# Queries and values of the next token tile projected between attention steps, with the ratio of sums on GpSimd

## Chip, cores and metric

The kernel runs on one core of a Trainium2 chip. The time is the device time of one execution, in microseconds. Three runs of the kernel before gave 947.82, 948.0 and 953.27; their median is 948.0.

## What is computed

One layer of a hybrid decoder for 512 prompt tokens and 64 sample tokens (8 sequences of 8), all float32. The part of the reference that matters here:

```python
mod = jax.nn.silu(c) @ w_ada + b_ada                      # adaLN: (shift, scale, gate) twice
h = rms_norm(x, g_pre_mix) * (1 + sc1) + sh1
zq, zk, zv, zu, zs = jnp.split(h @ w_in, ...)             # five column groups of 512
a = diff_attn_prompt(q, k, v, lam, slopes)                # 8 heads, two components of 32 each
#   s = q.k - slope * dist, masked;  p = softmax(s);  a = (p[0] - lam * p[1]) @ v
a = rms_norm(a, g_subln) * (1 - lam_init)
u = jax.nn.gelu(zu); vs = layer_norm(jax.nn.gelu(zs)); s_out = spatial_gating(u, vs)
mix = concatenate([a, s_out]) @ w_out                     # then sample attention, merge, 16 experts
```

## The kernel before, in words

The program is hand-scheduled: each engine has its own instruction stream, in order, tied to the others by semaphores. Four functions matter. `condition` norms x and runs adaLN round 0. `project` multiplies the normed tokens `hT` with the five column groups of `w_in`, in the order of `WIN_ORDER` (k, s, u, v, q), each for `NT` = 5 token tiles: four of 128 prompt tokens (8 matmuls of 128 x 512) and one of the 64 sample tokens (the 8 matmuls go to the lower and the upper half of the array's columns in turn, L776; VectorE adds the halves, L677 and L678). ScalarE copies each group out of PSUM, k, q and s groups are transposed or mixed behind it (`post`) and copied by VectorE (L667). adaLN rounds 1 and 2 (`ada_round`, L509, 64 short matmuls each, four 2 MB units of `w_ada`) run behind the groups named in `ADA_AFTER`. `attend_prompt` is prompt attention: 32 steps, tile i = 0 to 3 outside and head h = 0 to 7 inside; tile i has 128 (i + 1) keys. `attend_sample` is attention over the paged cache for the 8 sample sequences.

All large transfers go into a ring of slots of 2 MB (`L.ring`, 0 to 5). `STATIC` lists the weight units in the order in which SyncE's queue asks for them, with the slot of each (`ADA`, `WIN`); SyncE waits in order until the use before in the slot is over. `load_pages` (L794) on GpSimd gathers half a sequence's keys or values into a slot.

A step of attention, before: ScalarE has placed q of this tile into four zero-padded copies (`place_q`, L871), so that each of the two components is a matmul over all 128 partitions. TensorE writes two score banks (L958), two pairs in turn. VectorE adds the distance bias, takes the maximum and writes to one of three buffer pairs `pb` (L933), negates both maxima (L938); ScalarE takes exponentials with sums (L884). VectorE makes the ratio of the sums times -lambda (L909, L910) and combines the two components (L912), one head behind. TensorE transposes the weights two heads behind (L966), ScalarE copies them (L894), TensorE multiplies with the values three heads behind (L977), into bank 6 or 7 by tile. Behind head 4 of the next tile, `finish` divides, norms and stores the tile's eight heads in one go, VectorE waiting for a power on GpSimd (L816, L817). The order of the work in a step is that of the code:

```python
for n in range(N + 3):            # TensorE
    if n < N: ...                 # two score matmuls of head n, once s_read says the bank pair is free
    if 2 <= n < N + 2: ...        # transposes of head n - 2, once a_ready and at_done allow
    if n >= 3: ...                # value matmuls of head n - 3, once at_done allows
```

TensorE begins attention only when all five groups are projected (L947 to L949). GpSimd asks for six page loads at the start of attention (L846 to L851): keys of sequences 0 and 1, values of sequence 0, into slots 0 to 5.

Of the kernel before, what the change touches and what calls it, by code (L numbers as in the profile page):

```python
# [17 lines left out]
ALU = mybir.AluOpType  # L18
# [5 lines left out]
P = 128  # L24
# [5 lines left out]
NT = 5  # L30
# [126 lines left out]
def chain(eng, sem, start=0):  # L157
# [3 lines left out]
    def link(ins):  # L161
# [18 lines left out]
STATIC = [("ada", 0, j, s) for j, s in enumerate(ADA[0])] + [("win", 0, c, s) for c, s in enumerate(WIN)] + \  # L180
         [("ada", r, j, s) for r in (1, 2) for j, s in enumerate(ADA[r])]
# [14 lines left out]
def expert_slot(e, kind):  # L196


    q = 3 * e + kind
    slot = EXPERT[q % 8]  # L200
    return slot, STATIC_USES[slot] + (slot in W_OUT) + q // 8 + 1


class Program:
# [332 lines left out]
    def project(self, block):  # L537
# [5 lines left out]
        bn_done, rs_done, vs_ready, u_done, k_out, v_out, vs_out, ln_in = (  # L543
            self.sem(n) for n in ("bn_done", "rs_done", "vs_ready", "u_done", "k_out", "v_out", "vs_out", "ln_in"))
        dchain, pchain = self.sem("dve_chain_b"), self.sem("pool_chain_b")
        lam_in, lam_sum, lam_exp = (self.sem(n) for n in ("lam_in", "lam_sum", "lam_exp"))
        self.grp_done, self.evac_done, self.post_ev, self.posts = grp_done, evac_done, post_ev, 3 * NT
        summed = self.sem("summed")
        half = L.mix[0:NS, 3, 0:512]
# [3 lines left out]
        E = [L.at(L.X + 512 * i, 512) for i in range(4)]  # L553
        lng, lnb = L.at(L.V + 1536, 512), L.at(L.V + 2048, 512)
        groups = [(c, t) for c in WIN_ORDER for t in range(NT)]
        posts = [n for n, (c, t) in enumerate(groups) if c in "skq"]
# [3 lines left out]
        v_o = [o["v_prompt"][0, 0, t * P:(t + 1) * P].rearrange("t h d -> t (h d)") for t in range(4)] + \  # L560
            [o["v_sample"][0].rearrange("b t h d -> (b t) (h d)")]
# [8 lines left out]
        def _(sp):  # L570
# [10 lines left out]
            sp.wait_ge(self.mod_out, 16 * 2)  # L581
            sp.wait_ge(self.mod_outs, 16 * 8)
# [26 lines left out]
        def _(act):  # L609
            for n, (c, t) in enumerate(groups):  # L610
                r = rows(t)
                if c == "q" and t == 0:
                    act.wait_ge(lam_sum, 1)
                    act.activation(self.lam[:, 130:132], self.lam[:, 128:130], ACT.Exp).then_inc(lam_exp, 1)
# [4 lines left out]
                if n >= 4:  # L619

                    cb, tb = groups[n - 4]
                    if cb in "skq":
                        act.wait_ge(post_done, posts_to(n - 4))
# [8 lines left out]
                elif c == "v":  # L632
                    if t == 0:
                        act.wait_ge(post_done, posts_to(s0 + 4))
# [1756 lines left out]
```

## Time and profile before

| | us |
|---|---|
| median of three runs | 948.0 |
| the execution that was profiled | 947.89 |
| its span | 946.2 |
| TensorE busy in the span | 841.9 |
| VectorE busy | 346.4 |
| ScalarE busy | 208.9 |
| GpSimd busy | 118.8 |
| granted clock of TensorE, mean | 0.94 of full |
| bytes moved | 249.15 MB, 263 GB/s |

The span is what the hardware profiler saw of one execution, from the first to the last instruction; the time of the same execution is 1.7 us longer. Busy time of TensorE contains matmuls at a reduced clock. Condition takes about the first 40 us, projection goes to about 227, prompt attention to 334, sample attention to some 500, and merge and experts take the rest.

### The profile page before, as it was taken

Reading aid. Unit: us, or ns where it says so; the run is one execution under the profiler, and the core shown is the slowest. Engines: PE = TensorE matmul, PEld = TensorE weight load, DVE = VectorE, ACT = ScalarE, POOL = GpSimd, SP = SyncE. Lnnn points to the kernel's source line nnn. Section 1 sums busy time; section 2 is a strip of 40 time slices with the busy share of each in tenths; the row PEclk is TensorE's granted clock in tenths of the full one; section 3 lists DMA queues with packets and bytes.
Section 4 is the critical chain, followed back from the end, with each engine's and each line's share of the span. In section 5 each row is a group of like instructions: output and inputs, shape, how many; then the busy total and the mean of one; then the engine's idle time right before and its main releaser. Section 6 shows DMA issues by size and latency. Waiting matters only on the chain. (4 is left out here: it accounts for less than half of the span.)

```text
span 946.2 us, 12198 instructions
## 1 busy us (share of the span) xinstructions
PE 841.9 (89%) x4720; PEld 436.2 (46%) x4720; DVE 346.4 (37%) x843; ACT 208.9 (22%) x436; POOL 118.8 (13%) x190
## 2 busy tenths in 40 slices
PE   4699999997789679999988999479999999999995
PEld 3244444333555455665654455344444444444431
DVE  2304332104778545555451364442103011101137
ACT  4001001103666324333330211110101111101122
POOL 1300000002200112222120010001000000000044
PEclk8899999999779879999998998669999999999998
DMA  8996203635910047999797951508888999999973
GB/s 312 365 306 246 89 17 112 259 147 183 410 42 1 1 164 285 413 417 428 298 367 263 340 217 34 200 23 354 335 340 325 401 425 401 396 428 381 409 281 119
DMA packets 36709, 249.15 MB, mean 263 GB/s; under 512 B 4377, under 2 KB 5785, under 8 KB 23218
## 3 DMA queue, kind: packets, MB, share of 16 engines
q1 hardware_dynamic: 22834, 155.17, 41.8%
q0 software_dynamic: 9376, 81.47, 22.0%
q10 hardware_dynamic: 4448, 11.82, 3.8%
q8 instruction: 34, 0.56, 0.2%
q14 instruction: 17, 0.14, 0.0%
HBM read 231.91 MB, written 16.53 MB: 263 GB/s over the span
## 5 line engine op out<-in xcount | busy, mean ns | idle before, releaser
L770 PE MATMUL ps<-sb 128*128 128x512 f32 x320 | 142.8, 602 | 1.8 <-DVE sb L410 1.8
L2054 PE MATMUL ps<-sb 128*128 128x512 f32 (+1 forms) x256 | 112.9, 594 | 0.0
L770 PEld LDWEIGHTS ps<-sb 128*128 128x128 f32 x320 | 60.1, 192 | 75.7 <-issue 74.0
L1206 PE MATMUL ps<-sb 128*128 128x128 f32 x512 | 66.1, 284 | 18.8 <-ACT sb L1075 9.3
L1206 PEld LDWEIGHTS ps<-sb 128*128 128x128 f32 x512 | 57.6, 145 | 32.4 <-issue 18.3
L1978 DVE TENSOR_TENSOR sb<-sb,ps 128x512 f32<-128x512 f32 (+1 forms) x16 | 10.9, 684 | 160.3 <-PE ps L2054 87.1
L2044 PE MATMUL ps<-sb 128*128 128x512 f32 x144 | 66.4, 616 | 1.0 <-ACT sb L1896 0.9
L2079 PE MATMUL ps<-sb 128*128 128x512 f32 x144 | 63.5, 594 | 0.0
L1726 PE MATMUL ps<-sb 128*128 128x512 f32 x128 | 58.4, 616 | 3.9 <-DVE sb L1485 3.9
L2054 PEld LDWEIGHTS ps<-sb 128*128 128x128 f32 (+1 forms) x256 | 42.0, 167 | 34.0 <-issue 34.0
L958 PE MATMUL ps<-sb 128*128 128x128 f32 (+3 forms) x128 | 50.1, 526 | 3.2 <-ACT sb L871 3.2
L2051 PE MATMUL ps<-sb 128*64 128x512 f32 x112 | 49.6, 595 | 0.0
L1122 DVE COPY sb<-ps 128x512 f32<-128x512 f32 x64 | 41.2, 686 | 21.0 <-PE ps L1206 20.6
L1873 POOL DMA_INDIRECT sb<-h_rows,ints x16 | 15.0, 938 | 249.0 <-PE ps L2016 209.6
L884 ACT ACTIVATE sb<-sb 128x128 f32<-128x128 f32 (+3 forms) x64 | 35.4, 554 | 40.1 <-DVE sb L938 39.9
L2044 PEld LDWEIGHTS ps<-sb 128*128 128x128 f32 x144 | 27.6, 197 | 33.6 <-issue 31.7
L1075 ACT ACTIVATE sb<-ps 128x512 f32<-128x512 f32 x64 | 34.9, 595 | 33.9 <-PE ps L1206 33.5
L1726 PEld LDWEIGHTS ps<-sb 128*128 128x128 f32 x128 | 24.9, 198 | 34.5 <-issue 32.3
L2079 PEld LDWEIGHTS ps<-sb 128*128 128x128 f32 x144 | 26.7, 190 | 30.3 <-issue 30.1
L1989 DVE COPY sb<-ps 128x512 f32<-128x512 f32 (+1 forms) x16 | 11.1, 692 | 73.7 <-PE ps L2079 56.2
L1219 PE MATMUL ps<-sb 128*32 128x512 f32 (+1 forms) x320 | 36.5, 530 | 0.0
L933 DVE CUSTOM_DVE_ANT_0 sb<-ps,sb 128x128 f32<-128x128 f32 (+3 forms) x64 | 30.0, 489 | 14.7 <-PE ps L958 14.0
(297 smaller groups left out, 1018.6 us busy)
## 6 DMA issues: line engine op xcount, KB each, us to landing
sb<-in_w_gate SPq DMA_DIRECT2D x16, 2048.0 KB, 19.4
sb<-in_w_up SPq DMA_DIRECT2D x16, 2048.0 KB, 9.5
sb<-in_w_down SPq DMA_DIRECT2D x16, 2048.0 KB, 14.2
sb<-in_w_ada SPq DMA_DIRECT2D x12, 2048.0 KB, 15.5
sb<-in_w_in SPq DMA_DIRECT2D x5, 2048.0 KB, 24.6
y_rows<-sb SPq DMA_DIRECT2D x9, 512.0 KB, 15.5
sb<-in_w_out SPq DMA_DIRECT2D x2, 2048.0 KB, 21.2
sb<-in_x_prompt SPq DMA_DIRECT2D x4, 512.0 KB, 5.1
```

The costliest lines, as they stand in the source:

```text
L770: last = pe.matmul(PS[:, n % 4, :], L.hT[:, k, t * P:t * P + P], w[:, k, :], start=k == 0, stop=k == KC - 1)
L884: act.activation(pb[n % 3][j][:, 0:w], pb[n % 3][j][:, 0:w], ACT.Exp, bias=nm[:, q:q + 1], accum_out=sums[:, q:q + 1]).then_inc(exp_done, 1)
L958: pe.matmul(PS[:, 2 * (n % 2) + j, 0:P * (i + 1)], qz[i % 2][:, h // 2, 2 * (h % 2) + j, :], L.kT[:, h // 2, 0:P * (i + 1)], start=True, s ...
L1075: act.activation(kt[ch % 2][:, h, :], PS[:, h, :], ACT.Copy).then_inc(kt_act, 1)
L1122: dve.tensor_copy(kt[ch % 2][:, h, :], PS[:, h, :]).then_inc(kt_dve, 1)
L1206: last = pe.transpose(PS[:, h, P * g:P * g + P], kp[:, 4 * (ch % 2) + g, P * h:P * h + P], L.cst("ident"))
L1219: last = pe.matmul(bank[32 * h:32 * h + 32, 0:512 if ch < 4 else NS], qst[par][:, h, :], rhs, start=True, stop=True)
L1726: last = pe.matmul(PS[:, proj_bank(i, c), :], mixT[i % 2][:, k, :], w[:, k, :], start=k == 0, stop=k == KC - 1)
L2044: last = pe.matmul(PS[:, 0, :], x[:, k, :], w_gate[:, k, :], start=k == 0, stop=k == KC - 1)
L2051: last = pe.matmul(PS[n:P, 0, :], x[:, k, :], w_gate[:, k, :], start=k == 0, stop=k == KC - 1)
L2054: last = pe.matmul(PS[0:n, 1, :], x[:, k, :], w_up[:, k, :], start=k == 0, stop=k == KC - 1)
L2079: last = pe.matmul(PS[:, 5 + c, :], hT[:, k, :], w[:, k, 512 * c:512 * c + 512], start=k == 0, stop=k == FC - 1)
```

## The change

Projection keeps k, s and u; adaLN rounds 1 and 2 move up behind groups s2 and u1, with their own order of ring slots, and the weights of v and q are loaded behind them. Groups q and v move into `attend_prompt`. Tile 0 is projected ahead of the first head; q of tile t = i + 1 is spread over steps 0 to 2 of the eight heads of tile i, transposed in step 3, and v of tile t over steps 4 to 7 (`beside`, `product`, `turn`). All of these go through PSUM bank 7 (`bank_of`); values now gather in bank 6 alone. Value outputs are stored by SyncE's queue instead of ScalarE's.

The scores read the 32 partitions of q and k of one component directly, so `place_q` is gone. VectorE computes bias minus score and its minimum, which is the negated maximum, so the negation is gone, and ScalarE's exponential takes a scale of -1. The ratio of the sums is made by GpSimd, with three small operations. The combination is two heads behind instead of one, transposes three and value matmuls four, and there are four buffer pairs, which lie in ring slot 3. The norm of a tile is spread over heads 3, 4 and 5 of the next. The work on page numbers, distance bias and lambda sums moves from group v0 to u2. Of the six page loads three are asked for at the start of attention, slots 2 and 5 near its end, and slot 3 when the last value matmul is done.

```diff
-ADA = [[0, 1, 2, 3], [3, 4, 5, 0], [3, 4, 5, 0]]
-WIN = [4, 5, 0, 1, 2]
+ADA = [[0, 1, 2, 3], [1, 2, 3, 4], [1, 2, 3, 4]]
...
-ADA_AFTER = [("v", 2), ("q", 2)]
+ADA_AFTER = [("s", 2), ("u", 1)]
...
+STATIC = [("ada", 0, j, s) for j, s in enumerate(ADA[0])] + [("win", 0, c, s) for c, s in enumerate(WIN[:3])] + \
+         [("ada", r, j, s) for r in (1, 2) for j, s in enumerate(ADA[r])] + \
+         [("win", 0, 3 + c, s) for c, s in enumerate(WIN[3:])]
+ATTEND_SLOT = 3
...
+    return 3 * NT + len(BESIDE) * t + (c == "v")
...
+    t, k = n // H + 1, n % H
+    if n >= 4 * H:
+        return []
+    return [[("q", t, 0), ("q", t, 1)], [("q", t, 2)], [("q", t, 3)], [("turn", t, 0)],
+            [("v", t, 0)], [("v", t, 1)], [("v", t, 2)], [("v", t, 3)]][k]
...
+        slot = L.ring[ATTEND_SLOT]
+        pb = [[slot[:, 1024 * i + 512 * j:1024 * i + 512 * j + 512] for j in range(2)] for i in range(4)]
+        at = [self.E[2 + i].rearrange("p (b q) -> p b q", b=4) for i in range(2)]
...
-        qz = [L.at(n0 + 2048 * i, 2048).rearrange("p (h g q) -> p h g q", h=HP, g=4) for i in range(2)]
...
+        def bank_of(c, t):
+            return 6 if (c, t) == ("v", 0) else 7
...
+            pool.wait_ge(self.lam_sum, 1)
+            pool.wait_ge(grp_done, 3 * NT)
+            self.load_pages(pool, self.ck, 0, 0, K_SLOT[0][0], 0)
             pool.wait_ge(self.ada_done, 3)
-            pool.wait_ge(self.grp_done, 5 * NT)
-            for k, (cache, b, slots) in enumerate(((self.ck, 0, K_SLOT[0]), (self.ck, 1, K_SLOT[1]),
-                                                   (self.cv, 0, V_SLOT))):
-                for half in range(2):
-                    self.load_pages(pool, cache, b, half, slots[half], 2 * k + half)
+            self.load_pages(pool, self.ck, 0, 1, K_SLOT[0][1], 1)
+            self.load_pages(pool, self.cv, 0, 0, V_SLOT[0], 2)
...
+            for m in range(N):
+                q = 2 * m
+                pool.wait_ge(exp_done, q + 2)
+                link(pool.tensor_tensor(cf[:, q:q + 1], sums[:, q + 1:q + 2], minus, ALU.pow))
+                link(pool.tensor_tensor(cf[:, q:q + 1], cf[:, q:q + 1], sums[:, q:q + 1], ALU.mult))
+                if m == 0:
+                    pool.wait_ge(lam_made, 1)
+                pool.tensor_tensor(cf[:, q:q + 1], cf[:, q:q + 1], lam[:, 133:134], ALU.mult).then_inc(cf_ready, 1)
+                if m % H == 3 and m > H:
+                    pool.wait_ge(ss_ready, m // H)
+                    self.power(pool, link, ss, H, P, 1.0 / DV, ss_power)
+                if m == N - 4:
+                    pool.wait_ge(grp_done, group_at("q", 4) + 1)
+                    self.load_pages(pool, self.ck, 1, 0, K_SLOT[1][0], 3)
+            pool.wait_ge(grp_done, group_at("v", 4) + 1)
+            self.load_pages(pool, self.cv, 0, 1, V_SLOT[1], 4)
+            pool.wait_ge(pv_done, N)
+            self.load_pages(pool, self.ck, 1, 1, K_SLOT[1][1], 5)
...
-            place_q(0)
...
+            def project(c, t):
+                r, src = rows(t), PS[0:rows(t), bank_of(c, t), :]
+                act.wait_ge(grp_done, group_at(c, t) + 1)
+                if t == 4:
+                    act.wait_ge(self.summed, 4 + (c == "v"))
+                if c == "q":
...
+                    act.activation(E[t % 2][0:r], src, ACT.Copy, scale=DQK ** -0.5).then_inc(evac_done, 1)
...
+            for n in range(N + 3):
                 if n < N:
-                    act.wait_ge(m_ready, n + 1)
                     w = P * (work[n][0] + 1)
                     for j in range(2):
                         q = 2 * n + j
-                        act.activation(pb[n % 3][j][:, 0:w], pb[n % 3][j][:, 0:w], ACT.Exp, bias=nm[:, q:q + 1],
-                                       accum_out=sums[:, q:q + 1]).then_inc(exp_done, 1)
-                if n % H == 3 and n // H < 3:
-                    place_q(n // H + 1)
-                if n >= 2:
-                    m = n - 2
+                        act.wait_ge(s_read, q + 1)
+                        act.activation(pb[n % 4][j][:, 0:w], pb[n % 4][j][:, 0:w], ACT.Exp, bias=nm[:, q:q + 1],
+                                       scale=-1.0, accum_out=sums[:, q:q + 1]).then_inc(exp_done, 1)
+                if n >= 3:
+                    m = n - 3
...
+                for c, t, part in beside(n):
+                    if c != "turn" and part == 3:
+                        project(c, t)
...
+            def turned(t):
+                r = rows(t)
+                dve.wait_ge(post_done, 2 * NT + t + 1)
+                dve.tensor_copy(L.qT[:, :, t * P:t * P + r],
+                                PS[:, 7, :].rearrange("p (h t) -> p h t", h=HP)[:, :, 0:r]).then_inc(post_ev, 1)
...
-                dve.wait_ge(exp_done, 2 * m + 2)
-                link(dve.reciprocal(cf[:, q:q + 1], sums[:, q + 1:q + 2]))
-                link(dve.scalar_tensor_tensor(cf[:, q:q + 1], sums[:, q:q + 1], lam[:, 133:134], cf[:, q:q + 1],
-                                              ALU.mult, ALU.mult))
+                p1, p2 = pb[m % 4][0][:, 0:w], pb[m % 4][1][:, 0:w]
+                dve.wait_ge(cf_ready, m + 1)
                 dve.scalar_tensor_tensor(p1, p2, cf[:, q:q + 1], p1, ALU.mult, ALU.add).then_inc(a_ready, 1)
...
-                        dve.tensor_tensor_reduce(out=pb[n % 3][j][:, 0:w], in0=PS[:, 2 * (n % 2) + j, 0:w],
-                                                 in1=self.dist_bias[:, h, 384 - P * i:512], scale=1.0, scalar=-3e38,
-                                                 op0=ALU.add, op1=ALU.max,
-                                                 accum_out=mx[:, q + j:q + j + 1]).then_inc(s_read, 1)
-                    dve.wait_ge(s_read, 2 * n + 2)
-                    dve.tensor_scalar_mul(nm[:, q:q + 2], mx[:, q:q + 2], -1.0).then_inc(m_ready, 1)
-                if n >= 1:
-                    weights(n - 1)
-                if n % H == 4 and n // H >= 1:
-                    finish(n // H - 1)
-            finish(3)
+                        dve.tensor_tensor_reduce(out=pb[n % 4][j][:, 0:w], in0=PS[:, 2 * (n % 2) + j, 0:w],
+                                                 in1=self.dist_bias[:, h, 384 - P * i:512], scale=-1.0, scalar=3e38,
+                                                 op0=ALU.add, op1=ALU.min,
+                                                 accum_out=nm[:, q + j:q + j + 1]).then_inc(s_read, 1)
+                if n >= 2:
+                    weights(n - 2)
+                for c, t, part in beside(n):
+                    if c == "turn":
+                        turned(t)
+                    elif t == 4 and part == 3:
+                        summed(c)
+                if n < N and n >= H:
+                    if n % H == 3:
+                        taken(n // H - 1)
+                    if n % H == 4:
+                        squares(n // H - 1)
+                    if n % H == 5:
+                        normed(n // H - 1)
...
+            def product(c, t, part):
+                number = WIN_ORDER.index(c)
+                w = L.ring[WIN[number]].rearrange("p (k n) -> p k n", k=KC)
+                bank = bank_of(c, t)
+                if part == 0:
+                    if t == 0:
+                        pe.wait_ge(self.ring_full[WIN[number]], 16 * fills("win", 0, number))
+                    else:
+                        pe.wait_ge(post_ev, 2 * NT + t + (c == "v"))
+                    if c == "q" and t >= 2:
+                        pe.wait_ge(evac_done, group_at("v", t - 1) + 1)
+                if t < 4:
+                    for k in (2 * part, 2 * part + 1):
+                        last = pe.matmul(PS[:, bank, :], L.hT[:, k, t * P:t * P + P], w[:, k, :],
+                                         start=k == 0, stop=k == KC - 1)
+                else:
+                    for c0, k in ((0, part), (NS, part + KC // 2)):
+                        last = pe.matmul(PS[c0:c0 + NS, bank, :], L.hT[:, k, SEQ:TOK], w[:, k, :],
+                                         start=part == 0, stop=part == KC // 2 - 1)
+                if part == 3:
+                    last.then_inc(grp_done, 1)
...
+            def turn(t):
+                r = rows(t)
+                pe.wait_ge(evac_done, group_at("q", t) + 1)
+                for h in range(HP):
+                    last = pe.transpose(PS[:, 7, P * h:P * h + r], E[t % 2][0:r, P * h:P * h + P],
+                                        L.cst("ident", r)[:, 0:r])
+                last.then_inc(post_done, 1)
             pe.wait_ge(self.mod_sb, 9)
-            for n in range(N + 3):
+            for part in range(4):
+                product("q", 0, part)
+            for part in range(4):
+                product("v", 0, part)
+            turn(0)
...
+                        pe.wait_ge(post_ev, 2 * NT + i + 1)
                     for j in range(2):
-                        pe.matmul(PS[:, 2 * (n % 2) + j, 0:P * (i + 1)], qz[i % 2][:, h // 2, 2 * (h % 2) + j, :],
-                                  L.kT[:, h // 2, 0:P * (i + 1)], start=True, stop=True).then_inc(s_done, 1)
-                if 2 <= n < N + 2:
-                    m = n - 2
+                        r = 32 * (2 * (h % 2) + j)
+                        pe.matmul(PS[:, 2 * (n % 2) + j, 0:P * (i + 1)], L.qT[r:r + 32, h // 2, P * i:P * i + P],
+                                  L.kT[r:r + 32, h // 2, 0:P * (i + 1)], start=True, stop=True).then_inc(s_done, 1)
+                if 3 <= n < N + 3:
...
+                for c, t, part in beside(n):
+                    if c == "turn":
+                        turn(t)
+                    else:
+                        product(c, t, part)
+                if n >= 4:
...
+                        pe.wait_ge(evac_done, group_at("v", i) + 1)
+                        if i:
+                            pe.wait_ge(o_read, i)
```

## Rows read from the trace of the kernel before

**Rows 1.** The page: span and count of instructions.
```profile
span 946.2 us, 12198 instructions
```

**Rows 2.** TensorE's timeline: start, length (us), line, operation, count [idle before]; projection.
```profile
98.16 7.13 PE L770 MATMUL ps<-sb 128*128 128x512 f32 x16
...
145.75 20.87 PE L770 MATMUL ps<-sb 128*128 128x512 f32 x48
166.55 7.05 PE L509 MATMUL ps<-sb 128*9 128x512 f32 x64
...
180.60 3.65 PE L776 MATMUL ps<-sb 128*64 128x512 f32 x16
...
198.02 0.60 PE L752 MATMUL ps<-sb 128*128 128x128 f32 x4
...
229.91 2.90 PE L958 MATMUL ps<-sb 128*128 128x128 f32 x12 [3.20 <-ACT sb L871]
```

**Rows 3.** Windows: stretch, length, busy PE, PEld, DVE, ACT, POOL; PEclk, DMA, GB/s.
```profile
229.91:327.76 97.85, 81.11 (x528) 52.37 (x528) 72.88 (x274) 55.76 (x172) 12.46 (x18) 0.85 0.35 139
293.65:309.31 15.66, 15.66 (x113) 9.46 (x111) 13.52 (x40) 9.79 (x25) 0.09 (x1) 1.00 0.00 1
```

**Rows 4.** Waits of TensorE in attention: us in total, times, longest.
```profile
PE ps L966 <- DVE sb L912: 8.7, 6, 3.9
PE ps L977 <- ACT sb L894: 7.8, 7, 2.4
```

**Rows 5.** TensorE's timeline in attention, heads with 128, 256 and 512 keys.
```profile
242.90 0.74 PE L958 MATMUL ps<-sb 128*128 128x128 f32 x4
...
244.27 1.13 PE L958 MATMUL ps<-sb 128*128 128x256 f32 x4
245.24 0.27 PE L966 MATMUL ps<-sb 128*128 128x128 f32 x1
245.51 0.34 PE L977 MATMUL ps<-sb 128*64 128x64 f32 x4
...
306.06 1.98 PE L958 MATMUL ps<-sb 128*128 128x512 f32 x4
307.89 0.60 PE L966 MATMUL ps<-sb 128*128 128x128 f32 x4
308.42 0.97 PE L977 MATMUL ps<-sb 128*64 128x64 f32 x16
309.31 1.98 PE L958 MATMUL ps<-sb 128*128 128x512 f32 x4
```

**Rows 6.** Windows behind attention and in sample attention, columns as in rows 3.
```profile
327.76:335.97 8.21, 0.01 (x2) 0.03 (x1) 3.66 (x7) 0.00 (x0) 1.83 (x2) 0.74 0.00 0
...
290.00:336.00 46.00, 32.92 (x249) 20.52 (x248) 30.22 (x86) 18.54 (x47) 3.66 (x4) 0.88 0.00 1
380.00:460.00 80.00, 74.39 (x954) 48.51 (x952) 44.22 (x108) 30.09 (x53) 19.78 (x34) 1.00 1.00 417
```

**Rows 7.** TensorE's timeline in sample attention: eight passes on four column quarters.
```profile
380.38 1.06 PE L1219 MATMUL ps<-sb 128*32 128x512 f32 x8
```

**Rows 8.** Groups by form in attention: busy us, mean ns | idle before, releaser.
```profile
L884 ACT ACTIVATE sb<-sb 128x512 f32<-128x512 f32 x16 | 11.4, 714 | 16.4 <-DVE sb L938 16.4
L933 DVE CUSTOM_DVE_ANT_0 sb<-ps,sb 128x512 f32<-128x512 f32 x16 | 10.9, 690 | 5.1 <-PE ps L958 4.7
L912 DVE SCALAR_TENSOR_TENSOR sb<-sb 128x512 f32<-128x512 f32 x8 | 6.0, 752 | 0.3
L894 ACT ACTIVATE sb<-ps 128x512 f32<-128x512 f32 x8 | 4.5, 576 | 1.2 <-PE ps L966 1.2
```

**Rows 9.** Groups by form, GpSimd, whole span.
```profile
L801 POOL DMA_INDIRECT sb<-in_cache_k,ints x16 | 15.9, 994 | 13.6 <-POOL ints L798 12.4 <-issue 1.2
...
L330 POOL TENSOR_TENSOR sb<-sb 128x1 f32<-128x1 f32 x4 | 2.2, 552 | 0.3
...
L600 POOL TENSOR_SCALAR sb<-sb 128x1 f32<-128x1 f32 x4 | 0.8, 190 | 61.3 <-DVE sb L685 61.3
```

More of the change, by code:

```diff
@@ L552, in project @@
         k_outs = [k_out] + [self.sem(f"k_out{i}") for i in range(1, 4)]
-        E = [L.at(L.X + 512 * i, 512) for i in range(4)]
+        E = self.E = [L.at(L.X + 512 * i, 512) for i in range(4)]
         lng, lnb = L.at(L.V + 1536, 512), L.at(L.V + 2048, 512)
-        groups = [(c, t) for c in WIN_ORDER for t in range(NT)]
-        posts = [n for n, (c, t) in enumerate(groups) if c in "skq"]
+        groups = [(c, t) for c in WIN_ORDER[:3] for t in range(NT)]
+        posts = [n for n, (c, t) in enumerate(groups) if c in "sk"]
         mv = self.stats[:, 8:10]
@@ L727, in _ @@
                     post(n - 1)
-            post(len(groups) - 1)
         @block.tensor
@@ L840, in attend_prompt, with _ @@
         N = len(work)
+        E = self.E
+        v_o = [o["v_prompt"][0, 0, t * P:(t + 1) * P].rearrange("t h d -> t (h d)") for t in range(4)] + \
+            [o["v_sample"][0].rearrange("b t h d -> (b t) (h d)")]
+        def bank_of(c, t):
+            return 6 if (c, t) == ("v", 0) else 7
+        @block.sync
+        def _(sp):
+            for t in range(NT):
+                sp.wait_ge(evac_done, group_at("v", t) + 1)
+                sp.dma_start(v_o[t], L.v[0:rows(t), t, :]).then_inc(v_out, 16)
+            sp.wait_ge(v_out, 16 * NT)
+            sp.wait_ge(self.mod_out, 16 * 2)
+            sp.wait_ge(self.mod_outs, 16 * 8)
         @block.gpsimd
@@ L859, in _ @@
                 pool.dma_start(unused[:, WIDE - 2, 2, cols], L.mix[0:HALF, 4, 0:512]).then_inc(zeroed, 16)
-            for i in range(4):
-                pool.wait_ge(ss_ready, i + 1)
-                self.power(pool, link, ss, H, P, 1.0 / DV, ss_power)
+            pool.wait_ge(self.mod_sb, 9)
+            pool.memset(minus, -1.0).then_inc(minus_set, 1)
+            pool.wait_ge(minus_set, 1)
+            for m in range(N):
[16 more added lines that the diff above has]
+            self.load_pages(pool, self.ck, 1, 1, K_SLOT[1][1], 5)
+            pool.wait_ge(ss_ready, 4)
+            self.power(pool, link, ss, H, P, 1.0 / DV, ss_power)
             pool.wait_ge(zeroed, 64)
@@ L951, in _ @@
+            turn(0)
+            for n in range(N + 4):
                 if n < N:
                     i, h = work[n]
+                    if n == 0:
+                        pe.wait_ge(evac_done, 3 * NT)
                     if n >= 2:
```

149 lines of the change are left out of this document (75 added, 74 removed).

## The prediction

> **What bounds the kernel now.** I began with the span [rows 1] and then read TensorE's timeline through the projection and prompt attention, the only two stages that the diff touches. Up to the end of column group q TensorE does not stop: a full group (one column group, one token tile) takes 6.93 us, a third of the 20.8 between the starts at 145.75 and 166.55; a group of the 64 sample tokens 3.65 us, a transposition of q 0.6 us, an adaLN round 7.0 us [rows 2]. The first score matmul stands at 229.91. From there to the last value matmul, at 327.76, attention takes 97.85 us; TensorE is busy for 81.1 of them, at a mean granted clock of 0.85, and VectorE for 72.9 [rows 3]. So two things cost time there: TensorE waits (for VectorE's weights and for ScalarE's copies, 16.5 us together [rows 4]), and after such waits it runs part of the work at 1.2 GHz instead of 2.4. In the stretch where the clock is 1.00, TensorE is busy all of the time: 15.66 of 15.66 us [rows 3]. Attention is therefore TensorE's as soon as nothing stalls it, and the question is how much work TensorE has after the change.
>
> **TensorE's own work in attention, at full clock.** By starts of neighbouring rows at 1.00 [rows 5]: the two scores of a head take 0.74 us at 128 keys, 0.97 at 256, 1.83 at 512; by the half way between, 1.40 at 384. Transposes take 0.27 at one block and 0.53 at four; value matmuls 0.3 (of 0.34 with their modelled end) and 0.89; the two tiles between go by even steps. Four tiles of 8 heads: scores 8 x 4.94 = 39.5, transposes 8 x 1.6 = 12.8, values 8 x 2.4 = 19.0. Sum 71 us, against the 97.85 that it takes now: 27 us are stall and low clock.
>
> **Ahead of attention.** Groups u3 and u4 end at 145.75 today [rows 2]. Both adaLN rounds now run ahead of that point: 2 x 7.0 gives 159.7. They need their weights: each unit is 2.1 MB, and the queue moves 417 GB/s when it is full [rows 6], 5 us a unit. Round 1 takes the place at which s3 starts today, 98.2. Round 2's four units are asked for when it ends, at 105, and take 20 us, to 125 or so. From the start of s3 to the end of u4 it is 47.6 us today, of which u2 to u4 are 2 x 6.93 + 3.65 and a mixing of 1, 18.5: so TensorE comes to round 2 at 105 + 29 = 134. Some 8 us of slack. The weights of q are asked for at the end of round 2, 141, with nothing ahead in the queue but v's; needed at 159.7, so hidden with 10 us to spare. If that cover went, each late unit would cost up to 5 us. Then q0 and v0, 13.9 us, the transposition 0.6, VectorE's copy 0.7 and two hand-overs of 0.3: the first scores start at about 175.2, 54.7 us earlier than now. This also removes the q placing on ScalarE, whose place is the 3.2 us before 229.91 [rows 2].
>
> **What is moved into attention.** Six full groups (q and v of tiles 1 to 3), 41.6 us; two sample groups, 7.3; four transpositions by starts, some 2. Sum 51 us. With 71 this is 122 us of TensorE work between the first score and the last value. For the seams I add 5 us, an estimate: 28 parts each begin behind small matmuls and show 0.1 us of a weight load, and the last four steps drain as now.
>
> **Scores without placed q.** A score now reads 32 partitions, and the two of a head read different quarters of the array's rows and write different banks. No row of before has two matmuls on different row quarters. One bound: they run one after the other, as now: nothing gained. Other bound: as matmuls on different column quarters do, eight passes of 512 columns in 1.06 us, where two matmuls on the full array, four passes, take 1.83 [rows 5, 7]; likewise the 16 records of a sample group, on column halves, take half the time of a full group [rows 2]. With fewer keys the four weight loads of a head hold it at the 0.74 that 128 keys take already. So 0.74, 0.76, 0.9, 1.06 in place of 0.74, 0.97, 1.40, 1.83: 8 x 1.48 = 11.8 us less. I take this one: the column rows show the array running separate quarters at once. The end for the range keeps the other.
> The Trainium skill ("TensorE: Matmul & The Clock Gate", Part 3 on packing small matmuls) gives 3.07 times for four row tiles of 32 rows; by that the two scores would share their time much as the column rows have it. Against the change it says ("TensorEngine Tiling (Array Packing)", Key Properties) that a change of tiling mode drains the engine. Every head already switches between full and half-column matmuls, and [rows 5] has that in the prices.
>
> **VectorE, ScalarE, GpSimd.** Per head at 512 keys VectorE keeps two score reads of 0.69 and one combination of 0.75 [rows 8], with gaps 2.3 us; the reciprocal, the small product and the negation leave it. Eight heads: 18.4; with ten operations more of 512 columns at 0.69 (the copy of qT, four for the sample sums, five for the head norm) and small ones, 26 us. TensorE in the same eight heads of the last tile: 8 x (1.06 + 0.53 + 0.89) + 7.3 + 0.6 = 27.7. Close, but under; in the other tiles far under. ScalarE: two exponentials of 0.71, a copy of 0.58 and an evacuation as long every fourth head [rows 8], some 2.2 us a head. GpSimd: a power of 0.55 and two products of 0.2 with their hand-overs, 1.3 us a head [rows 9]. The ratio is ready about 5 us after the head's first score, and the combination, two heads later, asks for it at 8 or more; a load of pages in GpSimd's queue holds it 2 us longer [rows 9], still covered. Cost of the ratio on GpSimd: nothing; if the cover went, 1.3 us a head, 40 in all at the most.
> Bank 7 carries every moved group. After a group's last part TensorE still has values, the next scores and transposes, 1.3 to 3.2 us, and ScalarE's evacuation needs 0.8 of it; the head norm is spread over three heads, so the stalls of four heads [rows 4] end, and with them the low clock.
>
> **Behind attention.** The tail (8.2 us to the first transposes of the sample part [rows 6]) keeps its operations. GpSimd's last page load sits ahead of the norm's power, 2 us beside VectorE's 2.4: hidden. Three loads of pages move from the start of attention to its end. DMA is idle for the last 46 us now [rows 6], so slots 2 and 5 land before the sample part or with it, and slot 3, first read for the second half of the second sequence, at its start; the sample part's own rate of 417 GB/s between 380 and 460 says that bytes left over for it would cost 5 us a load. 4.2 MB ahead of the bias table may hold VectorE: 1 us. All later stages start by as much earlier, since none of their loads is asked for before.
>
> **Sum.** 122 - 11.8 + 5 = 115 us of attention from 175.2: end at 290, 37.5 earlier than 327.76; less 1 for the table. 946.2 - 36.5 = 909.7 of span. The execution profiled took 947.9 us, 1.7 more than its span, and the median of the runs is 948.0, so the two agree: 911 us.
>
> **Rivals.** (a) *The two scores stay serial*: 122 + 5 = 127, end at 302, 25 us gained: 923. For it: no row shows row quarters at once. (b) *Hand-over through bank 7*: ScalarE takes exp(n) and the copy ahead of the evacuation, and TensorE waits at eight evacuations and four transpositions, 1 to 1.5 us each, 12 to 16 on top of (a): 937. For it: in-order queues. Against: the 1.3 us of other work in between. (c) *The change of place buys nothing*: weights or ratio late enough to eat the 25 to 37 us, 947. That wants 5 late units or 1 us at every head. Against it: [rows 6, 9]. (d) *The clock*: with 32 of 128 rows in use in the scores the granted clock stays at 1.2 GHz. Each us of TensorE work at that level takes two. All of it: 122 more, against 25 gained, 1045 us. From 25 of the 122 us at the low level on, one fifth, it is slower than before. For it: the mean of 0.85 now [rows 3]; against: that follows waits, and products of full height lie between the scores.
>
> **How the numbers follow.** Chances: forecast 0.48, (a) 0.32, (b) 0.10, (c) 0.05, (d) 0.05. 911 us. The range goes from the forecast without seams and table (905, less 2 for waits that I count and that may vanish) to (a) with 3 us more: 903 to 926. Within 1% (about what a measurement can tell) means 938.5 to 957.5: (c), a little. Faster 0.9, same 0.05, slower 0.05.
>
> **What the profile after would show.** First score row near 175; last value row near 290 (302 for (a)); the granted clock of the stretch between at 0.97 or more (0.7 or less for (d)); TensorE busy over 95% of it; the scores of a head at 512 keys 1.1 us apart from the transposes (1.8 for (a)); no wait of TensorE for ScalarE's evacuations over 5 us in total (12 or more for (b)); none of VectorE for GpSimd's ratio; the sample part unchanged in length. Wrong would be the forecast if VectorE were busy over 95% of the last tile, or a projection waited for in_w_in or in_w_ada.

## The result, and the profile after

| | before | after |
|---|---|---|
| median, us | 947.9 (947.2 to 953.3, 4 runs) | 912.1 (909.8 to 914.0, 4 runs) |
| execution profiled: time / span, us | 947.9 / 946.2 | 909.8 / 907.8 |
| mean granted clock | 0.94 | 0.953 |

The ratio is 0.961, with a 95% interval of 0.957 to 0.965. Two later measurements of the same kernel, with the kernel before beside it each time, gave 904.9 and 906.9 (ratios 0.954 and 0.956). The prediction was 911.

TensorE's timeline at the three points that the prediction named: start, length, line, operation, count [idle before].

```profile
173.13 0.60 PE L1056 MATMUL ps<-sb 128*128 128x128 f32 x4
174.60 0.49 PE L1077 MATMUL ps<-sb 32*128 32x128 f32 x4 [0.87 <-DVE sb L952]
...
280.08 1.90 PE L1103 MATMUL ps<-sb 128*64 128x64 f32 x32
295.96 4.30 PE L1332 MATMUL ps<-sb 128*128 128x128 f32 x20 [13.98 <-PEq L282]
```

The first scores start at 174.60 (229.91 in [rows 2]) and the last value matmul ends at 281.98. Behind it stands the first disagreement with the forecast: a gap of 13.98 us, where the kernel before has 8.20 [rows 6]. Its releaser is TensorE's own sequencer at L282, the end of the block, and no data.

Windows of the kernel after (columns as in [rows 3]): all of attention, then the gap.

```profile
174.60:281.98 107.38, 106.24 (x672) 53.30 (x672) 59.04 (x186) 53.56 (x168) 39.75 (x106) 1.00 0.20 66
281.98:295.96 13.98, 0.01 (x1) 0.03 (x1) 3.65 (x6) 0.00 (x0) 3.53 (x4) 0.65 0.71 279
```

TensorE is busy for 106.2 of 107.4 us (99%), at a granted clock of 1.00; before it was 81.1 of 97.9 at 0.85 [rows 3]. Its waits in that stretch, in us, times, longest, are three:

```profile
PE ps L1077 <- DVE sb L952: 0.9, 1, 0.9
PE ps L1056 <- ACT sb L912: 0.6, 1, 0.6
PE ps L1085 <- DVE sb L966: 0.4, 1, 0.4
```

against 16.5 us of [rows 4]. The stalls are gone, and the low clock with them.

Heads with 128, 256 and 512 keys in TensorE's timeline:

```profile
187.70 0.49 PE L1077 MATMUL ps<-sb 32*128 32x128 f32 x4
188.12 0.33 PE L1085 MATMUL ps<-sb 128*128 128x128 f32 x1
188.28 1.88 PE L1042 MATMUL ps<-sb 128*128 128x512 f32 x4
190.10 0.34 PE L1103 MATMUL ps<-sb 128*64 128x64 f32 x4
...
195.70 0.70 PE L1077 MATMUL ps<-sb 32*128 32x256 f32 x4
196.33 0.33 PE L1085 MATMUL ps<-sb 128*128 128x128 f32 x1
...
248.98 1.13 PE L1077 MATMUL ps<-sb 32*128 32x512 f32 x4
250.04 0.55 PE L1085 MATMUL ps<-sb 128*128 128x128 f32 x3
```

From start to next start the two scores of a head take 0.42, 0.63 and 1.06 us, where [rows 5] had 0.74, 0.97 and 1.83. The part of a moved group (L1042) takes 1.8 us and stands between the transposes and the values of other heads.

### The profile page after: what moved, and what is told of

It is laid out like the page before. It is cut to its first block and busy times, and to the rows that moved or that the text cites. A ratio compares the mean times of both kernels' runs of the same rounds, so it can differ in the third digit from the quotient of the medians.

```text
span 907.8 us, 12182 instructions
## 1 busy us (share of the span) xinstructions
PE 815.8 (90%) x4720; PEld 415.2 (46%) x4720; DVE 327.6 (36%) x747; ACT 199.5 (22%) x420; POOL 151.6 (17%) x287
## 5 line engine op out<-in xcount | busy, mean ns | idle before, releaser
L1332 PEld LDWEIGHTS ps<-sb 128*128 128x128 f32 x512 | 57.1, 144 | 37.7 <-issue 24.1
L1042 PE MATMUL ps<-sb 128*128 128x512 f32 x128 | 59.2, 597 | 0.1
L768 PEld LDWEIGHTS ps<-sb 128*128 128x128 f32 x192 | 36.2, 193 | 45.7 <-issue 44.2
L2170 PEld LDWEIGHTS ps<-sb 128*128 128x128 f32 x144 | 27.6, 197 | 33.6 <-issue 31.7
L1852 PEld LDWEIGHTS ps<-sb 128*128 128x128 f32 x128 | 24.9, 198 | 34.7 <-issue 32.4
L2205 PEld LDWEIGHTS ps<-sb 128*128 128x128 f32 x144 | 26.7, 190 | 30.3 <-issue 30.1
```

The source lines that it names most:

```text
L768: last = pe.matmul(PS[:, n % 4, :], L.hT[:, k, t * P:t * P + P], w[:, k, :], start=k == 0, stop=k == KC - 1)
L1042: last = pe.matmul(PS[:, bank, :], L.hT[:, k, t * P:t * P + P], w[:, k, :], start=k == 0, stop=k == KC - 1)
L1332: last = pe.transpose(PS[:, h, P * g:P * g + P], kp[:, 4 * (ch % 2) + g, P * h:P * h + P], L.cst("ident"))
L1852: last = pe.matmul(PS[:, proj_bank(i, c), :], mixT[i % 2][:, k, :], w[:, k, :], start=k == 0, stop=k == KC - 1)
L2170: last = pe.matmul(PS[:, 0, :], x[:, k, :], w_gate[:, k, :], start=k == 0, stop=k == KC - 1)
L2205: last = pe.matmul(PS[:, 5 + c, :], hT[:, k, :], w[:, k, 512 * c:512 * c + 512], start=k == 0, stop=k == FC - 1)
```

## The experiments

Where no range stands beside a time, it is of one run; the others are medians. "Gap" is the time from the end of the last value matmul to the first transposes of the sample part; "attention" is from the first score matmul to the end of the last value matmul.

### The gap behind attention: loads, stores or traffic

**e1_loads_behind.** GpSimd's last two page loads are issued behind the end of the block.

```diff
-            self.load_pages(pool, self.cv, 0, 1, V_SLOT[1], 4)
             pool.wait_ge(pv_done, N)
-            self.load_pages(pool, self.ck, 1, 1, K_SLOT[1][1], 5)
...
+            self.load_pages(pool, self.cv, 0, 1, V_SLOT[1], 4)    # attend_sample, GpSimd
+            self.load_pages(pool, self.ck, 1, 1, K_SLOT[1][1], 5)
             refill(0, 0, True, 6)
```

> The last two page loads of prompt attention (slots 5 and 3) are asked for behind the barrier, ahead of the first refill of sample attention. Theory L (the barrier ahead of sample attention ends only when GpSimd's page loads have landed): the gap between the last value matmul and the first transposes of sample attention falls from 13.98 us to 8.2 as before, the span from 907.8 to 902 to 904. Theory V (SyncE's wait for the last value store holds the barrier, its bytes queued beside the loads) also gives 8 to 10 here; only the next run tells it from L. Theory N (the gap is the semaphore clearing or code of the longer program): it stays at 14 and the span at 907 or more. If both loads come too late for sequences 0 and 1, TensorE waits in sample attention and gives some of it back: 2 to 5 us.

Measured: 899.9 us (899.1 to 903.3, 4 runs), ratio 0.950 (0.947 to 0.952). The gap row of its timeline:

```profile
290.43 4.22 PE L1332 MATMUL ps<-sb 128*128 128x128 f32 x24 [8.20 <-PEq L282]
```

The gap is 8.20 us again, to a hundredth that of the kernel before. The span of the profiled execution, 898.4 us, is shorter than the 902 to 904 that I expected; the kernel after itself ran 5 to 7 us faster in its two later measurements (e5_after_again, e12_after_third), so only e11_loads_again, which has both kernels on one chip, prices the edit.

**e2_no_store_wait.** SyncE's wait for the value stores is taken out of the block; ScalarE waits for them at the end of sample attention.

```diff
-            sp.wait_ge(v_out, 16 * NT)          # attend_prompt, SyncE
...
+            act.wait_ge(self.v_out, 16 * NT)    # attend_sample, ScalarE, last
```

> SyncE's wait for the five value stores moves from the end of prompt attention to the end of sample attention (on ScalarE); the page loads stay where they are. Theory V: the gap behind the last value matmul falls from 14.0 to 8 to 9 us. Theory L: it stays at 14.0, within 0.5.

Measured: 904.9 us. The gap stays:

```profile
296.66 5.27 PE L1333 MATMUL ps<-sb 128*128 128x128 f32 x24 [14.46 <-PEq L282]
```

So it is not the stores.

**e3_other_traffic.** As e1_loads_behind, but SyncE asks for two units of w_ada, 4.2 MB that nothing uses, when the last value matmul is done, and GpSimd waits for them behind the end of the block.

```diff
+            sp.wait_ge(pv_done, N)
+            for s in (3, 5):
+                sp.dma_start(ring[s], a["w_ada"]...).then_inc(self.spare, 16)
...
+            pool.wait_ge(self.spare, 32)        # attend_sample, ahead of the two page loads
```

> As e1, and SyncE's queue asks for 2 x 2 MB of w_ada into the same slots 3 and 5 when the last value matmul is done; nothing waits for them before the barrier, GpSimd waits for them behind it. The loaded values are not used. Theory L (only GpSimd's own transfers hold the barrier): the gap is 8.2 to 8.7. Theory C (any traffic on the DMA engines at that moment holds the barrier, since something that the barrier needs is queued behind it): 13 to 17 us, about 10 us of transfer and the rest.

Measured: 905.2 us. Windows of its gap, then waits of TensorE and of GpSimd:

```profile
281.50:289.80 8.30, 0.00 (x0) 0.03 (x1) 3.66 (x6) 0.00 (x0) 1.85 (x2) 0.61 0.87 336
```

```profile
PE ps L1338 <- PEq L282: 8.3, 1, 8.3
```

```profile
POOL ints L795 <- DMA sb<-in_w_ada: 8.4, 1, 8.4
```

The DMA engines are 0.87 busy through the gap, and it is still 8.3 us: the transfers run on past the end of the block and hold nobody but the wait that names them. Bytes in flight on SyncE's queue do not lengthen it; page loads in flight on GpSimd's do. In the kernel after the engines fall idle shortly before TensorE goes on (windows of 1 us, last columns DMA share and GB/s):

```profile
291.00:292.00 1.00, 0.00 (x0) 0.00 (x0) 0.00 (x0) 0.00 (x0) 0.00 (x0) 0.50 0.95 410
292.00:293.00 1.00, 0.00 (x0) 0.00 (x0) 0.00 (x0) 0.00 (x0) 0.00 (x0) 0.50 0.24 98
293.00:294.00 1.00, 0.00 (x0) 0.00 (x0) 0.00 (x0) 0.00 (x0) 0.00 (x0) 0.50 0.00 0
```

VectorE's last work there ends at 288.0; the loads end at about 292.3, and TensorE starts 3.7 us later. The other profiles agree. In all nine that have the two loads ahead of the end of the block, TensorE starts 3 to 4 us after the DMA engines fall idle. The gap is 12.61 us in e8_ratio_vector, where GpSimd issues the value load 5.3 us before the last value matmul ends, 13.98 us in the kernel after (3.0 us before), and 15.92 us in e10_depth_before (2.2 us before). GpSimd's own instructions don't explain it: the last of them, the norm's power, ends 4.6 us behind the last value matmul in the kernel after and 4.5 us behind it in e1_loads_behind.

Two things stay open. The transfers of e3_other_traffic differ from the page loads in two ways, the engine that issues them and their kind (plain copies, and not gathers by an index in memory), and no run parts these. And what in the end of the block waits for the loads (`forget` clears semaphores and then meets at a barrier) was not taken apart.

### The scores on row quarters

**e4_one_quarter.** Both score matmuls of a head read the same 32 rows; the second component is therefore a copy of the first.

```diff
-                        r = 32 * (2 * (h % 2) + j)
+                        r = 64 * (h % 2)
```

> Both scores of a head read the same 32 partitions of q and k (the second component is computed as a copy of the first), all else as after. Theory Q (the two scores run together because they lie on different quarters of the array's rows): scores at 512 keys take 1.7 to 1.9 us from start to next start instead of 1.06, at 128 keys 0.6 to 0.8 instead of 0.42; prompt attention grows from 107.4 to 118 to 123 us. Theory K (a matmul over 32 partitions is cheaper by itself): 1.06 and 107.4 stay.

Measured: 920.5 us, attention 176.63 to 299.01, 122.4 us against 107.4, at a granted clock of 1.00.

```profile
285.22 1.98 PE L1077 MATMUL ps<-sb 32*128 32x512 f32 x4
287.13 0.66 PE L1085 MATMUL ps<-sb 128*128 128x128 f32 x4
```

The scores of a head take 1.91 us at 512 keys, 1.06 at 256 and 0.63 at 128, in place of 1.06, 0.63 and 0.42. The same instructions on the same number of rows, 15.0 us apart in all: the two quarters run side by side.

**e6_quarters_alone.** The kernel before with only this edit: scores from the 32 partitions, `place_q` gone.

```diff
-            place_q(0)
...
-                        pe.matmul(PS[:, 2 * (n % 2) + j, 0:P * (i + 1)], qz[i % 2][:, h // 2, 2 * (h % 2) + j, :],
-                                  L.kT[:, h // 2, 0:P * (i + 1)], ...)
+                        r = 32 * (2 * (h % 2) + j)
+                        pe.matmul(PS[:, 2 * (n % 2) + j, 0:P * (i + 1)], L.qT[r:r + 32, h // 2, P * i:P * i + P],
+                                  L.kT[r:r + 32, h // 2, 0:P * (i + 1)], ...)
```

> The kernel before with one part of the change: the scores read the 32 partitions of a component from qT, and the placing of q on ScalarE is gone. Projection stays ahead of attention. TensorE's own work falls by 15 us at full clock (the prices of after) and the start comes 2.5 us earlier. Theory B (VectorE and the one-head-behind chain bound the kernel before as soon as TensorE has less): attention goes from 97.85 to 88 to 94 us, 938 to 943 us. Theory T (TensorE's work bounds it): attention 82, 930 us.

Measured: 951.9 us (949.9 to 954.2, 10 runs), ratio 1.005 (1.003 to 1.007). An edit that takes 16 us of work (at full clock) from TensorE made the kernel 4 us slower. Attention goes from 228.26 to 333.27, 105.0 us, where the two theories had 88 to 94 and 82. A window over most of it, and TensorE's wait in all of it:

```profile
229.46:303.00 73.54, 63.70 (x329) 33.82 (x330) 51.61 (x214) 35.57 (x128) 11.29 (x17) 0.51 0.48 192
```

```profile
PE ps L962 <- DVE sb L909: 15.4, 6, 5.3
```

The granted clock is 0.51 over 73 us: TensorE runs at 1.2 GHz, and a transpose of one block takes 0.47 us in place of 0.27. Neither theory had this. The clock fell at about 231, behind waits of 1.70, 0.56, 0.69 and 1.54 us in the first heads, and came back at 309.46.

### The granted clock

**e7_all_ahead.** The kernel after, with q and v of all tiles projected ahead of the first head, in turn through four banks; `beside` gives nothing. Depth, quarters and GpSimd's ratio stay.

```diff
-    if n >= 4 * H:
-        return []
+    return []
...
-            for part in range(4):
-                product("q", 0, part)
...
+            for t in range(NT):
+                for part in range(4):
+                    product("q", t, part)
...
```

> The changed kernel with all tiles of q and v projected ahead of the first head (queries in banks 0 and 1, transposes in 2 and 3, values in 4 and 5); scores on quarters, four pairs, GpSimd's ratio, the spread norm stay. First scores at 226. TensorE has 57 us of work left in attention, VectorE 59. Theory I (projection between steps fills TensorE's idle time): attention is 64 to 74 us, the last value matmul at 290 to 300 instead of 282, 920 to 930 us. Theory J (with the other parts done the place of the projection gives nothing): last value matmul by 285, 908 to 915 us. The page loads still end in the tail: gap 12 to 14.

Measured: 936.3 us (932.5 to 939.7, 4 runs), ratio 0.988 (0.985 to 0.992); attention 223.94 to 312.17, 88.2 us, where theory I had 64 to 74 and theory J an end by 285: both missed. In the same measurement the kernel after took 904.9 us (e5_after_again), so the place of the projections is worth 31 us here. Windows from the end of the projections to the first transposes of the heads, on to the return of the clock, and to the last value matmul:

```profile
222.06:227.38 5.32, 1.42 (x16) 0.91 (x17) 3.28 (x17) 3.01 (x13) 1.40 (x4) 0.91 0.12 28
227.38:298.18 70.80, 70.64 (x364) 37.64 (x364) 42.94 (x145) 38.09 (x130) 29.19 (x85) 0.50 0.00 1
298.18:312.17 13.99, 13.10 (x149) 9.13 (x148) 9.61 (x21) 8.05 (x19) 8.65 (x18) 1.00 0.49 172
```

The fall still follows waits: TensorE is busy for 1.4 of the first 5.3 us (waits of 1.88, 0.58 and 1.44 us), and the clock drops between 226 and 227. What is new is that it does not come back: TensorE is then busy for 70.6 of 70.8 us and at 1.2 GHz all the while. At 298.18, in the last tile, it returns, and the last 14 us of the same kind of work run at 2.4 GHz; no run shows why there.

The kernel before, whose scores are 128 rows high, with no projections between them either, gets its clock back much sooner. Three of its stretches at the low clock, each from the end of a wait of TensorE (2.35, 1.96 and 3.88 us) to the return of the clock:

```profile
238.92:242.90 3.98, 3.98 (x23) 2.97 (x23) 2.19 (x14) 1.92 (x10) 1.04 (x2) 0.50 1.00 424
261.61:266.60 4.99, 4.99 (x25) 3.46 (x26) 3.37 (x16) 2.81 (x12) 0.00 (x0) 0.50 0.41 108
315.17:321.32 6.15, 6.15 (x24) 3.54 (x25) 3.07 (x10) 2.88 (x8) 0.00 (x0) 0.50 0.00 0
```

**e9_ahead_full_height.** The same with each score over all 128 rows of q and k. A score then is the sum over four components.

```diff
-                        r = 32 * (2 * (h % 2) + j)
-                        pe.matmul(..., L.qT[r:r + 32, h // 2, P * i:P * i + P], L.kT[r:r + 32, h // 2, 0:P * (i + 1)], ...)
+                        pe.matmul(..., L.qT[:, h // 2, P * i:P * i + P], L.kT[:, h // 2, 0:P * (i + 1)], ...)
```

> The kernel of e7_all_ahead (all projections ahead of the heads, nothing between them) with each score matmul over all 128 rows of q and k instead of over the 32 rows of its own component; both components of a head are then sums over four components, so the output is another. In e7_all_ahead TensorE ran without a gap from 229 to 298, at a granted clock of 0.50. Theory H (a matmul on 32 rows counts for little with what grants the clock, a matmul on 128 rows counts in full): the clock is 1.00 through the heads. The scores then take 39.5 us as in the kernel before, 15.8 more than on quarters, the rest some 20 us at full clock: attention ends about 60 to 68 us after the first scores, less than the 88 of e7_all_ahead although there is more to do. Theory S (the heads' short matmuls and transposes lose the clock whatever the height of the scores; only the long run of 512-column projection matmuls between them kept it): the clock stays at 0.50 for most of the stretch, and attention takes 110 to 125 us.

Measured: 927.4 us; attention 226.49 to 299.62. Windows of its first heads with the wait ahead of them, and of all of it:

```profile
224.60:230.10 5.50, 2.43 (x18) 2.10 (x18) 3.50 (x19) 3.01 (x13) 1.48 (x5) 1.00 0.12 27
226.49:299.62 73.13, 68.74 (x528) 45.60 (x528) 54.89 (x178) 48.86 (x160) 39.91 (x106) 1.00 0.10 35
```

73.1 us at a clock of 1.00, where the quarters took 88.2 us. The same transposes and value matmuls, one for one, run at 2.4 GHz throughout beside scores of 128 rows, and at 1.2 GHz for 71 of 88 us beside scores on quarters. My 60 to 68 was too low: TensorE's busy time alone is 68.7 us, and 4.4 us of waits come on top. Its start has waits of 1.88 and 1.19 us, much like e7's, and yet the clock did not fall; so e9 shows a clock that is kept, and the return of a lost one is shown by the kernel before. What differs between e7 and e9 is the height of the scores, that they no longer run in pairs, and that TensorE is busy for 2.4 of the first 5.5 us instead of 1.4 of 5.3; the runs don't part these.

### Depth, and the ratio on GpSimd

**e8_ratio_vector.** The ratio goes back to VectorE, right ahead of the combination.

```diff
-                link(pool.tensor_tensor(cf[:, q:q + 1], sums[:, q + 1:q + 2], minus, ALU.pow))
-                ... two products                                     # GpSimd
+                link(dve.reciprocal(cf[:, q:q + 1], sums[:, q + 1:q + 2]))
+                link(dve.scalar_tensor_tensor(cf[:, q:q + 1], sums[:, q:q + 1], lam[:, 133:134], cf[:, q:q + 1], ...))
```

> The ratio of the sums back on VectorE (reciprocal and one product of one column, in front of the combination), the combination still two heads behind. Theory F (VectorE has room: 59 us busy of 107): attention stays at 107.4, within 0.5, VectorE's busy time rises to 71. Theory G (VectorE is near the bound in the last tile): attention grows by 2 to 6 us, in heads 24 to 31.

Measured: 907.6 us; attention 112.8 us, 5.4 more than 107.4. The place where most of it goes, in its timeline and windows:

```profile
263.31 0.46 PE L1056 MATMUL ps<-sb 64*128 64x64 f32 x4 [1.10 <-ACT sb L907]
263.69 1.18 PE L1103 MATMUL ps<-sb 128*64 128x64 f32 x12
264.80 2.08 PE L1077 MATMUL ps<-sb 32*128 32x512 f32 x4
```

```profile
262.00:271.00 9.00, 7.90 (x48) 4.37 (x48) 7.61 (x20) 4.55 (x11) 0.05 (x1) 0.62 0.01 2
```

The wait is for ScalarE's evacuation of the sample group, which stands behind a sum by VectorE. Behind it TensorE runs at 1.2 GHz for 6 to 7 us; the kernel after waits 0.65 us at the same place and keeps its clock. In all of attention TensorE is busy for 109.7 us in place of 106.2 (the clock, 3.5 us) and idle for 3.1 in place of 1.1 (2.0 us). Size and place are those of theory G. The total, one run, can't be told from the 904.9 to 912.1 of the kernel after.

**e10_depth_before.** The kernel after with the combination one head behind, transposes two, values three; all else stays, the four buffer pairs too (the expectation says three).

```diff
-                if n >= 2:
-                    weights(n - 2)
+                if n >= 1:
+                    weights(n - 1)
...
```

> The kernel after with the depth of the kernel before: combination one head behind, transposes two behind, values three behind, three score buffer pairs; projections between the heads, quarters and GpSimd's ratio stay. Theory D (the greater depth carries part of the gain, since a ratio on GpSimd of about 1.0 us, 0.55 + 0.20 + 0.25 in the rows of after, stands between the exponentials and the combination): waits of PE's transposes for the weights appear, 0.3 to 1 us a head, 10 to 25 us in all, first at the short heads; attention 117 to 130 us against 107.4. Theory P (TensorE has the projections' 1.6 us of each step to stand on, and one head less of depth costs nothing until the last tile, where there is no projection): attention within 3 us of 107.4 but for waits in the last eight heads. If the gaps are there, a fall of the granted clock may follow them, and would double the cost of the heads it covers.

Measured: 923.4 us; attention 174.39 to 291.93, 117.5 us. Its waits and one of the three borders between tiles:

```profile
PE ps L1103 <- DVE sb L975: 6.5, 3, 2.4
```

```profile
209.59 0.46 PE L1103 MATMUL ps<-sb 128*64 128x64 f32 x8 [2.09 <-DVE sb L975]
```

No head waits for its weights: theory D's reason is wrong. TensorE waits 2 us at each border for VectorE to take the finished tile out of its bank, which I had left at head 3, one head late for this depth; 6.5 us of waits, and a mean clock of 0.96 over attention. The 117.5 us lie in theory D's range by luck, for another reason. The run shows that the shallower depth (combination one head behind) still covers GpSimd's ratio, and not what a well-placed shallower version would take.

### The kernel after again, and the better version

**e5_after_again.**

> The changed kernel once more, unchanged, beside the others of this call, since one of its four runs was 4 us slower than another and e2, whose prompt attention and tail are as long, ended 4.6 us earlier in span. If that was the chip and its memory, 903 to 912 us here with attention at 107.4 and the tail at 14.0.

Measured: 904.9 us (904.5 to 906.5, 4 runs); gap 13.9.

**e11_loads_again** and **e12_after_third**, on one chip.

> The kernel of e1_loads_behind again, on one chip with the kernel after beside it. Theory L (GpSimd's last two page loads hold the block's end by 5.8 us in after, and moved behind it they cost nothing elsewhere): 5 to 6 us below the kernel after on the same chip, so 899 us where after takes 905, ratio to before 0.949. Rival W (what the earlier start gives is taken back in the sample part, where the same pages are then waited for): less than 2 us below after.

> The kernel after, unchanged, beside e11_loads_again on the same chip: 904 to 912 us by its two measurements so far (912.05 and 904.89), attention 107.4 us and a gap of 13.9 to 14.0 us before the sample part in its profile whatever its total.

Measured: 900.3 us (898.3 to 902.7, 6 runs) and 906.9 us (904.5 to 910.6, 6 runs), ratios to before 0.949 (0.946 to 0.952) and 0.956 (0.953 to 0.959). The difference of the medians is 6.7 us, for the 5.6 us by which the gap is shorter (8.20 against 13.82). In the profiles the sample part up to its last long wait takes 162.3 us against 160.8, so at most some 1.5 us are given back there, within rival W's 2 but far from taking the gain. Moving two page loads behind the end of the block beats both kernels.

## Why the prediction was right, and where it was not

**Ahead of attention: right.** First scores at 174.60, forecast 175.2 (175.5 if each of the two hand-overs takes the 0.3). Both adaLN rounds run without a wait for their weights.

**Attention: right in its mechanism, 7.6 us too long.** 115 us were forecast, 107.4 measured. From starts to next starts of the timeline after, its parts against mine are: scores 23.6 (39.5 - 11.8 = 27.7); moved groups and transpositions 53.0 (51 + 5 for seams); transposes 12.3 (12.8); value matmuls 17.5 (19.0); waits 1.0 (0). Three terms were mis-sized. The *scores*: I let four weight loads hold a short head at the 0.74 us of the 128-key rows. The rows above show 0.42 at 128 keys and 0.63 at 256. The Trainium skill ("TensorE: Matmul & The Clock Gate", Part 3, The mechanism) states that a weight load overlaps running matmuls when its row group differs; the 0.42 agrees, and I had not drawn the consequence. The *seams*: a full group takes 7.3 us between the heads (43.8 us for six) instead of 6.93, so the seams cost 2 us, not 5. *Transposes and values* cost 2 us less than by the rows of before: a projection behind a transpose of one block starts 0.16 us after it (188.12 to 188.28) and not 0.27; the rest was not taken apart.

**Rival (a), serial scores: refuted** by e4_one_quarter, which is that rival made: 122.4 us of attention and 920.5 us in all, where I had 127 and 923. (No run has scores of 128 rows between moved projections; two of them took 1.83 us at 512 keys [rows 5], about the 1.91 of e4, so its time is an estimate for that case too.) **Rival (b), the hand-over through bank 7: absent**, 0.6 us of waits for ScalarE in all. **Rival (c)**: no weight was late, and TensorE never waited for a ratio; e8_ratio_vector gives the ratio's move a value of 5.4 us, most of it clock.

**Rival (d), the clock: absent in the kernel after, but its mechanism is real.** I gave it 0.05 and argued that the low clock follows waits. That holds for the fall (e6, e7, e8, e10 and the kernel before all have waits ahead of it) and not for the return: in e7_all_ahead TensorE worked without a wait for 71 us at 1.2 GHz. The second half of my argument, that products of full height lie between the scores, is what the runs bear out: with projections between the heads the clock was back 7 us after the wait in e8, and 5 and 6 us after two of the three waits in e10 (the third, 2.38 us long, did not lose it). In the kernel before, without them, the row quarters cost more than they save. That the kernel after keeps its clock has two parts, short waits (0.87 us at the most) and the work between; no run parts them.

**The tail: the step that failed.** "GpSimd's last page load sits ahead of the norm's power, 2 us beside VectorE's 2.4: hidden." The instruction was hidden; its transfer was not. The gap grew from 8.20 to 13.98 us because the end of the block came only after GpSimd's outstanding loads had landed (e1 against e2 and e3). I had asked whether the bytes come in time for their readers, and not who waits for the loads themselves.

**Why 911 fitted all the same.** The terms against the forecast: -0.6 at the start, -7.6 in attention, +5.8 in the gap. The sample part, 159.6 us before (335.97 to the wait at 495.53) and 160.7 after (295.96 to 456.64), gave the +1 that I had taken for the table; it is 158.9 and 160.8 in e5 and e12, so a single profile can't show that 1 us. Together they are 2.3 us below the forecast; the span, 907.8 against 909.7, is 1.9 below. Two errors of six to eight microseconds cancelled: that 911 came so near is luck, that it was faster by some 4% is not. The medians of 904.9 and 906.9 lie within the range. The profiled executions of the same kernel differ by 3.6 us (102.8 to 106.4) in a stretch behind sample attention that the change does not touch.

## To carry to other kernels

Work of full height between small matmuls did two things here: it covered the hand-overs (1.0 us of waits left of 16.5), and where a wait did cost the clock, the clock was back within 5 to 7 us and not after 71. Take it away only after looking at the granted clock of what is left. For a transfer asked for ahead of a block's end, look for who waits for the issuing queue, not only for who reads the bytes. Packing scores on row quarters wants a look at the clock as much as at the start-to-start time.

## What the hardware showed that I had not expected

- Matmuls on two row quarters run side by side in float32, their weight loads too: two scores in 1.06 us against 1.91 on one quarter (512 columns), 0.42 against 0.63 (128).
- Busy for 70.64 of 70.80 us, TensorE stayed at a granted clock of 0.50 with paired scores of 32 rows (e7). With scores of 128 rows beside the same transposes and value matmuls it kept 1.00 (e9), and in the kernel before it had its clock back after 4.0 to 6.2 us of gapless work.
- A wait of 1.10 us was followed by 6 to 7 us at 1.2 GHz (e8), one of 0.65 at the same place by none. The length of a wait alone does not decide it: 2.38 us in e10 and 1.88 us in e9 left the clock as it was.
- Page loads in flight on GpSimd's queue held the end of a block by 5.8 us; 4.2 MB of plain copies in flight on SyncE's queue did not hold it.
